# Slot 0 of a mixture-of-experts stage takes its tokens in pairs, in the down products and in the scatter

## The chip, the cores and the metric

The kernel runs on one core of a Trainium2 chip, in one launch. The metric is the device time of that launch in microseconds (us). Three runs of the kernel before took 1530.29, 1531.33 and 1532.8 us; the median is 1531.33 us. All numbers of the trace come from one profiled execution, which took 1531.39 us.

## The reference

Two layers of a transformer, 256 tokens of 1024 numbers, all in 32-bit floats. Each layer has a mixer (three kinds of attention); the first layer ends with a dense feed-forward block, the second with a mixture of eight experts, which is the part that matters here:

```python
def swiglu(h, w_gate_up, w_down):
    gt, up = jnp.split(h @ w_gate_up, 2, axis=-1)
    return (jax.nn.silu(gt) * up) @ w_down

def moe_swiglu(h, w_router, w_gate_up, w_down):
    ...
    logits = (t @ w_router).astype(jnp.float32)
    top_val, top_idx = lax.top_k(logits, TOP_K)          # TOP_K = 2 of 8
    top_w = jax.nn.softmax(top_val, axis=-1)
    ...
    for e in range(N_EXPERTS):
        y = y + combine[:, e:e + 1] * swiglu(t, w_gate_up[e], w_down[e])
```

An expert's hidden layer is 3584 wide. Its weights are 1024 x 7168 and 3584 x 1024 numbers, 44 MB; the eight of them are 352 MB, and every one is read once for each slot that works on it.

## The kernel before

**Slots.** After the router, the experts are worked on one after the other in slots. A slot is one expert with up to 96 tokens (three blocks of 32) or up to 64 (two blocks). `BLOCKS_AT = (3, 2, 3, 2, 3, 3, 2)` gives the blocks of the first seven slots; the others, in a loop, have two. A matmul with one-hot rows (`sel`) gathers a slot's tokens, and another (`selT`) scatters its result back.

**Slabs.** An expert's weights lie in memory as 42 slabs of 128 x 2048 numbers (1024 KB), in the order in which they are used. SyncE issues their transfers, in order, into a ring of 22 places (21 from slot 2 on). For slots 0 and 1 it issues one slab at a time (`single_slabs`, L683): the transfer of a slab waits on the semaphore `slab_used` until the slab 22 places before it has been used. From slot 2 on one transfer brings three slabs (L692). TensorE counts `slab_used` up with the last matmul that reads a slab.

**A slot on TensorE.** The order is written out in `expert`: gate and up products of stage 0 (8 slabs), for slot 0 then the gather of slot 1 (for the others the scatter of the slot before), gate and up of stage 1 (8), down of stage 0 (4), gate and up of stage 2 (8), down of stage 1 (4), gate and up of stage 3 (4), down of stage 2 (4), down of stage 3 (2). So 28 slabs are for gate and up, and 14 for down.

**Lanes.** A block of 32 tokens is a stationary tile of 128 x 32. Four such matmuls lie side by side in TensorE (lanes): lane g has columns 32g to 32g + 31, reads its own quarter of the slab's columns, and writes its own 32 partitions of the accumulator (`pa` for gate and up, `ps` for down). ScalarE applies SiLU (L1318), VectorE multiplies gate and up into `hs` (L1929) and transposes `hs` in 32 x 32 pieces into `hf` (L1933), which is the stationary operand of the down products.

**Pairs.** From slot 1 on, the down products take the first two blocks together: a stationary tile of 128 x 64, 512 moving columns instead of 256, and two such matmuls side by side (halves) instead of four lanes. A third block, where there is one, still goes in four lanes. The two ways need different layouts of `hs` and `hf` (`hidden_rows`, `gate_up`). With pairs, `down` takes two slabs at a time: first the pair's matmuls of both slabs, then the third block's of both, and only these last ones count `slab_used` up. Without pairs (slot 0) each slab is finished, all three blocks of it, before the next begins. The scatter has two forms in the same way: with pairs a contraction over 64 rows for the first two blocks and over 32 rows for the third; without, over 32 rows for each block. The result of slot 0 is scattered within slot 1 (`scatter_slot(1, ...)`, which asks `paired(0)`).

The function that decides is `paired(i)` at L441, called in `expert` and `choose` on VectorE, in `expert` on ScalarE, and in `down` (L2546) and `scatter_slot` (L2471) on TensorE.

Of the kernel before, what the change touches and what calls it, by code (L numbers as in the profile page):

```python
# [71 lines left out]
def blocks_of(i):  # L72
    return BLOCKS_AT[i] if type(i) is int and i < len(BLOCKS_AT) else FEW_BLOCKS
# [6 lines left out]
def is_first(i):  # L80
    return type(i) is int and i == 0


WIDE_BLOCKS, FEW_BLOCKS = 3, 2
# [89 lines left out]
def trunk(nc, x_in, mem_in, mix_norm_g, w_in, sb_q_g, sb_k_g, gla_a_up, gla_a_b, gla_o_g, ca_q_g,  # L174
# [10 lines left out]
    with ExitStack() as ctx:  # L185
# [254 lines left out]

        def paired(i):  # L441

            return not is_first(i)

        def half_rows(a, h):

# [518 lines left out]
        def _(act):  # L965
# [342 lines left out]
            def expert(i, blocks, blocks_ago, blocks_next):  # L1308
                used = i * EXP_SLABS + PRE

                if not is_first(i):
                    output(i, blocks_ago)
                for s in range(STEPS):
                    used += GU[s]
                    act.wait_ge(slab_used, used)
                    if s > 0 or not is_first(i):
                        act.wait_ge(e_turned, i * STEPS + s)
                    act.activation(hidden_rows(s, blocks, paired(i)), gate_up(s, 0, blocks, paired(i)),  # L1318
                                   ACT.Silu)\
                        .then_inc(e_silu, 1)  # L1320
                    used += DN[s - 1] if s > 0 else 0
# [14 lines left out]
        def _(dve):  # L1336
# [564 lines left out]
            def choose(i, blocks):  # L1901
                dve.wait_ge(selt_turned, i + 1)
                rows = [row_no[:, b:b + 1] for b in range(blocks)]
                for b, row in enumerate([pair_row] + rows[2:] if paired(i) else rows):
                    ins = dve.tensor_scalar(selT[:, b, :], ps[:, DM:DM + SEQ], row, None,
                                            ALU.is_equal)
                ins.then_inc(selt_ready, 1)
                name_positions(i + 1)
                if not is_first(i):
                    name_tokens(i + 1)  # L1910
# [7 lines left out]
            def expert(i, blocks, blocks_ago, blocks_next):  # L1918
                used = i * EXP_SLABS + PRE

                if not is_first(i):
                    output_lo(i, blocks_ago)
                for s in range(STEPS):
                    if s == 0 and is_first(i):
                        slot_tables()
                    used += GU[s]
                    dve.wait_ge(slab_used, used)
                    dve.wait_ge(e_silu, i * STEPS + (s + 1))
                    dve.tensor_tensor(hidden_rows(s, blocks, paired(i)), gate_up(s, 1, blocks, paired(i)),  # L1929
                                      hidden_rows(s, blocks, paired(i)), ALU.mult).then_inc(e_h, 1)  # L1930
                    dve.wait_ge(e_h, i * STEPS + (s + 1))
                    n = blocks * lanes_wide(s)
                    dve.transpose(hf[:, s % 2, 0:n], hs[:, 0:n]).then_inc(e_turned, 1)  # L1933
                    if s == 0:
                        if not is_first(i):
                            add_slot(i)
                        choose(i, blocks)
                    used += DN[s - 1] if s > 0 else 0
                turn_tokens(i + 1, blocks_next)
# [744 lines left out]
```

## Time and profile before

| what | value |
|---|---|
| median of three runs | 1531.33 us |
| the profiled execution | 1531.39 us, of which 1529.6 us between its first and its last instruction (the span) |
| slot 0 on TensorE | 729.0 to 839.9 us after the span's start |
| slot 1 on TensorE | 839.9 to 918.1 us |
| TensorE matmuls busy | 1500.2 us, 98% of the span |
| bytes moved by DMA | 482 MB, 315 GB/s over the span |

Times in the rows below are microseconds from the span's start. "Busy" for TensorE (PE) is the time in which at least one matmul was under way, so four lanes side by side count once. The trace has two records for each 32-bit matmul, and one for a matmul of type fp32r: where the program has 96 matmuls of a down stage, a row says x192. A name as "exp_raw" is the tile that holds the ring of slabs, and "exp_extra" is its 22nd place. "128*64 128x512" is a stationary tile of 128 x 64 and a moving one of 128 x 512.

### The profile page before, as it was taken

Reading aid. Unit: us, or ns where it says so; the run is one execution under the profiler, and the core shown is the slowest. Engines: PE = TensorE matmul, PEld = TensorE weight load, DVE = VectorE, ACT = ScalarE, POOL = GpSimd, SP = SyncE. Lnnn points to the kernel's source line nnn. Section 1 sums busy time; section 2 is a strip of 40 time slices with the busy share of each in tenths; the row PEclk is TensorE's granted clock in tenths of the full one; section 3 lists DMA queues with packets and bytes.
Section 4 is the critical chain, followed back from the end, with each engine's and each line's share of the span. In section 5 each row is a group of like instructions: output and inputs, shape, how many; then the busy total and the mean of one; then the engine's idle time right before and its main releaser. Section 6 shows DMA issues by size and latency. Waiting matters only on the chain.

```text
span 1529.6 us, 25846 instructions
## 1 busy us (share of the span) xinstructions
PE 1500.2 (98%) x11443; PEld 879.9 (58%) x11443; DVE 549.2 (36%) x675; ACT 431.8 (28%) x562; POOL 83.6 (5%) x126
## 2 busy tenths in 40 slices
PE   9999999999999999999999999999999999999878
PEld 7887888888888887887335333343333433433213
DVE  6655675655557664666301101001010110010101
ACT  7657653544445657453000000000000000000000
POOL 4211100200002110001000000000000000000000
PEclk9999999999999999999999999999999999999999
DMA  9655455665656554678999999999999999999996
GB/s 335 201 156 164 127 185 159 194 192 185 195 212 207 164 161 144 239 276 330 419 401 402 420 430 428 429 429 428 429 430 429 427 430 427 428 429 430 428 430 280
DMA packets 86415, 482.17 MB, mean 315 GB/s; under 512 B 11344, under 2 KB 13472, under 8 KB 64160
## 3 DMA queue, kind: packets, MB, share of 16 engines
q1 hardware_dynamic: 84784, 477.82, 80.3%
q0 software_dynamic: 1216, 2.17, 0.5%
q8 instruction: 90, 1.47, 0.4%
q10 hardware_dynamic: 304, 0.53, 0.1%
q14 instruction: 21, 0.17, 0.0%
HBM read 477.35 MB, written 3.15 MB: 314 GB/s over the span
## 4 chain that ended last, share of the span: by engine, by line
PE 89%; DMA 9%; DVE 1%; issue 0%; ACT 0%; DVEq 0%; SPq 0%; POOLq 0%
PE pa L2242 28%; PE ps L2242 19%; PE pa L2066 14%; PE pa L2068 13%; PE pa L2067 13%; DMA exp_raw<-in_moe_slabs 8%; PE ps L2236 0%; DMA w_raw<-in_w_mem_kv 0%; DMA gain<-in_mix_norm_g 0%; PE ps L1985 0%; PE ps L2415 0%; PE pa L2103 0%; PE ps L2392 0%; DVE r L1400 0%; PE ps L2025 0%
## 5 line engine op out<-in xcount | busy, mean ns | idle before, releaser
L2242 PE MATMUL pa<-exp_raw,xf 128*32 128x512 f32 (+1 forms) x5104 | 491.9, 542 | 16.6 <-DMA exp_raw<-in_moe_slabs 14.5
L2242 PEld LDWEIGHTS pa<-exp_raw,xf 128*32 128x32 f32 x5104 | 163.5, 110 | 326.1 <-issue 271.5
L1365 DVE TENSOR_TENSOR w_lo<-w_raw,w_hi 128x1024 fp32r<-128x1024 f32 x210 | 255.7, 1233 | 122.4 <-ACT w_hi L989 114.2
L989 ACT ACTIVATE w_hi<-w_raw 128x1024 fp32r<-128x1024 f32 (+1 forms) x212 | 220.1, 1053 | 130.1 <-PE pa L2068 117.6
L2242 PE MATMUL ps<-exp_raw,hf 128*32 128x256 f32 (+1 forms) x2032 | 246.7, 464 | 4.1 <-DMA exp_raw<-in_moe_slabs 4.0
L2066 PE MATMUL pa<-w_hi,r 128*128 128x512 f32 x600 | 239.7, 399 | 0.5 <-DVE r L1400 0.4
L1929 DVE TENSOR_TENSOR hs<-pa,hs 128x768 f32<-128x768 f32 (+3 forms) x32 | 23.7, 741 | 586.5 <-ACT hs L1318 586.5
L2067 PE MATMUL pa<-w_lo,r 128*128 128x512 f32 x600 | 234.0, 390 | 0.0
L2068 PE MATMUL pa<-w_hi,r 128*128 128x512 f32 x600 | 233.9, 390 | 0.0
L1318 ACT ACTIVATE hs<-pa 128x768 f32<-128x768 f32 (+3 forms) x32 | 20.4, 638 | 661.8 <-PE pa L2242 661.8
L2242 PEld LDWEIGHTS ps<-exp_raw,hf 128*32 128x32 f32 (+1 forms) x2032 | 91.6, 120 | 158.8 <-issue 128.3
L2066 PEld LDWEIGHTS pa<-w_hi,r 128*128 128x128 f32 x600 | 112.6, 188 | 27.9 <-issue 3.2
L2068 PEld LDWEIGHTS pa<-w_hi,r 128*128 128x128 f32 x600 | 112.6, 188 | 24.3
L2067 PEld LDWEIGHTS pa<-w_lo,r 128*128 128x128 f32 x600 | 112.8, 188 | 21.9
L2066 PE MATMUL pa<-w_hi,xt 128*128 128x512 f32 (+1 forms) x308 | 118.4, 384 | 0.3
L2068 PE MATMUL pa<-w_hi,xt 128*128 128x512 f32 (+1 forms) x308 | 116.6, 379 | 0.0
L2067 PE MATMUL pa<-w_lo,xt 128*128 128x512 f32 (+1 forms) x308 | 116.5, 378 | 0.0
L2066 PEld LDWEIGHTS pa<-w_hi,xt 128*128 128x128 f32 x308 | 57.9, 188 | 12.3 <-issue 1.5
L2068 PEld LDWEIGHTS pa<-w_hi,xt 128*128 128x128 f32 x308 | 57.9, 188 | 10.9
L2067 PEld LDWEIGHTS pa<-w_lo,xt 128*128 128x128 f32 x308 | 58.0, 188 | 10.3
L1914 DVE TENSOR_TENSOR yf<-ps,yf 128x768 fp32r<-128x768 f32 (+1 forms) x7 | 5.9, 844 | 85.3 <-ACT yf L1305 85.3
L1305 ACT ACTIVATE yf<-ps 128x768 fp32r<-128x768 f32 (+1 forms) x7 | 5.0, 719 | 93.3 <-PE ps L2242 93.3
(285 smaller groups left out, 856.4 us busy)
## 6 DMA issues: line engine op xcount, KB each, us to landing
exp_raw<-in_moe_slabs SPq DMA_DIRECT2D x82, 3072.0 KB, 31.0
exp_raw<-in_moe_slabs SPq DMA_DIRECT2D x86, 1024.0 KB, 8.6
w_raw<-in_w_in SPq DMA_DIRECT2D x104, 512.0 KB, 4.4
w_raw<-in_ff_w_gate_up SPq DMA_DIRECT2D x44, 512.0 KB, 4.5
w_raw<-in_ff_w_down SPq DMA_DIRECT2D x22, 512.0 KB, 4.1
w_raw<-in_w_out SPq DMA_DIRECT2D x16, 512.0 KB, 4.2
w_raw<-in_w_mem_kv SPq DMA_DIRECT2D x15, 512.0 KB, 4.6
w_raw<-in_w_br_sb SPq DMA_DIRECT2D x8, 512.0 KB, 3.3
```

The lines of the kernel that those rows point to most:

```text
L989: act.activation(dst, raw, ACT.Copy).then_inc(hi_ready, 1)
L1305: act.activation(yf[:, 0, 0:blocks * OUT], ps[:, 0:blocks * OUT], ACT.Copy)\
L1318: act.activation(hidden_rows(s, blocks, paired(i)), gate_up(s, 0, blocks, paired(i)), ACT.Silu)\
L1365: dve.tensor_tensor(dst, raw, hi.bitcast(F32), ALU.subtract)\
L1914: dve.tensor_tensor(yf[:, 1, 0:blocks * OUT], ps[:, 0:blocks * OUT], yf[:, 0, 0:blocks * OUT].bitcast(F32), ALU.subtract)\
L1929: dve.tensor_tensor(hidden_rows(s, blocks, paired(i)), gate_up(s, 1, blocks, paired(i)), hidden_rows(s, blocks, paired(i)), ALU.mult).then ...
L2066: pe.matmul(dst, hi, m_hi, start=first, stop=False)
L2067: pe.matmul(dst, hi, m_lo, start=False, stop=False)
L2068: return pe.matmul(dst, lo, m_hi, start=False, stop=last)
L2242: return pe.matmul(dst, a, b, start=start, stop=stop, skip_group_check=True)
```

## The change

One line, in the function that says for which slots tokens go in pairs:

```diff
         def paired(i):
 
-            return not is_first(i)
+            return blocks_of(i) >= FEW_BLOCKS
```

`FEW_BLOCKS` is 2 and every slot has two or three blocks, so the function is now true for all slots. It was false for slot 0 alone, which has three blocks.

On TensorE, the first down stage of slot 0 (4 slabs; "64x512" and "32x256" are the shapes of the result in the accumulator):

```order
 L2242 MATMUL pa<-exp_raw,xf 32x512 x96
-L2242 MATMUL ps<-exp_raw,hf 32x256 x48
-L2242 MATMUL ps<-exp_extra,hf 32x256 x24
-L2242 MATMUL ps<-exp_raw,hf 32x256 x24
+L2242 MATMUL ps<-exp_raw,hf 64x512 x8
+L2242 MATMUL ps<-exp_raw,hf 32x256 x16
+L2242 MATMUL ps<-exp_extra,hf 64x512 x4
+L2242 MATMUL ps<-exp_raw,hf 64x512 x4
+L2242 MATMUL ps<-exp_extra,hf 32x256 x8
+L2242 MATMUL ps<-exp_raw,hf 32x256 x8
 L2242 MATMUL pa<-exp_raw,xf 32x512 x96
```

Where 24 matmuls finished one slab, 8 of the pair form now go through two slabs, and then 16 of the lane form through the same two. The other down stages of slot 0 change alike: 336 matmuls become 56 of the pair form and 112 of the lane form, in seven groups of two slabs.

On TensorE, the scatter of slot 0's result, which stands in slot 1 between its gate and up stages:

```order
 L2613 TENSOR_LOAD slot_i
 L2613 ISA x2
 L2242 MATMUL pa<-exp_raw,xf 32x512 x64
-L2242 MATMUL ps<-yf,selT 128x256 x48
+L2242 MATMUL ps<-yf,selT 128x256 x32
 L2242 MATMUL pa<-exp_raw,xf 32x512 x16
 L2242 MATMUL ps<-ident,small 128x128 x2
```

It has 32 matmuls instead of 48: 16 contract over 64 rows, 16 over 32 rows. On ScalarE and VectorE the SiLU and the product of slot 0 write their 768 (or 384) columns in another order, with the same count of instructions, and `choose` builds `selT` for slot 0 in two instructions instead of three. GpSimd and SyncE run the same instructions as before, in the same order.

## Rows read from the trace of the kernel before

**Rows 1.** The page: GB/s moved in 40 equal slices of the span.

```profile
GB/s 335 201 156 164 127 185 159 194 192 185 195 212 207 164 161 144 239 276 330 419 401 402 420 430 428 429 429 428 429 430 429 427 430 427 428 429 430 428 430 280
```

**Rows 2.** Stretches: slot 0 after its first stage, early slot 1, later.

```profile
core 0: us, PE busy (x) PEld busy (x) DVE busy (x) ACT busy (x) POOL busy (x), PEclk, DMA share, GB/s
754.00:841.00 87.00, 87.00 (x1248) 40.30 (x1240) 5.60 (x7) 2.92 (x4) 0.00 (x0) 1.00 1.00 403
841.00:884.00 43.00, 43.00 (x400) 13.95 (x396) 7.03 (x11) 1.20 (x3) 0.00 (x0) 1.00 1.01 420
884.00:1420.00 536.00, 532.86 (x5214) 192.34 (x5208) 59.86 (x91) 17.74 (x27) 0.00 (x0) 1.00 1.00 429
```

**Rows 3.** SyncE's DMA issues, 754 to 841: waits in us, times, longest.

```profile
SPq L683 <- PE pa L2242: 44.2, 20, 4.7
SPq L683 <- PE ps L2242: 29.7, 14, 2.2
```

**Rows 4.** DMA issues, us to landing: 762-770, 804-824, 824-842, 842-884.

```profile
exp_raw<-in_moe_slabs SPq DMA_DIRECT2D x3, 1024.0 KB, 6.3
...
exp_raw<-in_moe_slabs SPq DMA_DIRECT2D x8, 1024.0 KB, 7.4
...
exp_raw<-in_moe_slabs SPq DMA_DIRECT2D x6, 1024.0 KB, 8.1
...
exp_raw<-in_moe_slabs SPq DMA_DIRECT2D x20, 1024.0 KB, 14.0
```

**Rows 5.** Timeline of TensorE, slots 0 and 1: start, us, instruction.

```profile
772.72 5.36 PE L2242 MATMUL ps<-exp_raw,hf 128*32 128x256 f32 x96
...
783.08 20.78 PE L2242 MATMUL pa<-exp_raw,xf 128*32 128x512 f32 x192
803.68 10.54 PE L2242 MATMUL ps<-exp_raw,hf 128*32 128x256 f32 x192
...
824.40 10.54 PE L2242 MATMUL ps<-exp_raw,hf 128*32 128x256 f32 x192
...
839.94 13.92 PE L2242 MATMUL pa<-exp_raw,xf 128*32 128x512 f32 x128
853.79 1.69 PE L2242 MATMUL ps<-yf,selT 32*128 32x256 f32 x48
855.42 3.64 PE L2242 MATMUL pa<-exp_raw,xf 128*32 128x512 f32 x32
```

**Rows 6.** Timeline of TensorE, slots 2 and 3.

```profile
962.38 10.97 PE L2242 MATMUL ps<-exp_raw,hf 128*64 128x512 f32 x96
973.16 20.78 PE L2242 MATMUL pa<-exp_raw,xf 128*32 128x512 f32 x192
993.87 10.97 PE L2242 MATMUL ps<-exp_raw,hf 128*64 128x512 f32 x96
...
1016.86 16.41 PE L2242 MATMUL ps<-exp_raw,hf 128*64 128x512 f32 x144
1033.09 13.92 PE L2242 MATMUL pa<-exp_raw,xf 128*32 128x512 f32 x128
1046.93 2.29 PE L2242 MATMUL ps<-yf,selT 64*128 64x256 f32 x32
1049.15 3.64 PE L2242 MATMUL pa<-exp_raw,xf 128*32 128x512 f32 x32
```

**Rows 7.** TensorE's waits for slabs, 729 to 1410, then to 1529.

```profile
PE pa L2242 <- DMA exp_raw<-in_moe_slabs: 1.1, 1, 1.1
...
PE pa L2242 <- DMA exp_raw<-in_moe_slabs: 13.4, 10, 3.3
PE ps L2242 <- DMA exp_raw<-in_moe_slabs: 4.0, 3, 1.8
```

**Rows 8.** Timeline of VectorE: the product of slot 0 and of slot 2.

```profile
773.89 0.96 DVE L1929 TENSOR_TENSOR hs<-pa,hs 128x768 f32<-128x768 f32 x1 [19.91 <-ACT hs L1318]
...
963.42 0.96 DVE L1929 TENSOR_TENSOR hs<-pa,hs 128x768 f32<-128x768 f32 x1 [15.23 <-ACT hs L1318]
```

## The prediction, made before the changed kernel ran

> **What bounds the kernel now.** First the page's row of bytes moved [rows 1]. It falls into two parts. In the first 19 slices (19 x 38.2 = 727 us) the core moves 127 to 335 GB/s; from the 20th on it moves 401 to 430 GB/s, but for the last. So the expert stage reads weights as fast as they come, and TensorE, which the table shows busy for 98% of the span, is not what sets the end there: in the last slots it waits for slabs, 13.4 + 4.0 us after 1410, and 1.1 us once before that [rows 7].
>
> Then the same view by stretches that I chose from the timeline [rows 2]. From 884 to 1420 the rate is 429 GB/s. From 841 to 884 (slot 1, still one slab per transfer) it is 420. In slot 0, from 754 to 841, it is only 403. One slab is 1.049 MB, so it takes 2.50 us at 420 GB/s and 2.60 us at 403.
>
> Why is slot 0 slower? SyncE's waits [rows 3]: in these 87 us each of the 34 transfers was held until TensorE had used the slab 22 places before, 44.2 + 29.7 us in all. The timeline of TensorE [rows 5] gives the pace of these releases. Gate and up of a stage takes 803.68 - 783.08 = 20.60 us for 8 slabs, 2.58 us each. The first down stage takes 783.08 - 772.72 = 10.36 us for 4 slabs, 2.59 us each. The last two take 839.94 - 824.40 = 15.54 us for 6 slabs, 2.59 us again. 1.049 MB in 2.59 us is 405 GB/s, which is what slot 0 moves. So in slot 0 the transfers go at TensorE's pace, and from slot 1 on, where a two-block slot uses slabs faster (839.94 to 853.79 for 8), at their own.
>
> The time from issue to landing says how much stands in the queue [rows 4]. It is 6.3 us at its lowest, 7.4 and 8.1 us later in slot 0, and 14.0 us in slot 1. I read 6.3 us as a transfer with nothing ahead of it; then q = 8.1 - 6.3 = 1.8 us at most stands ahead at the end of slot 0, and 7.7 us in slot 1. From there on TensorE can be late by some microseconds and no transfer would be late. What is lost in slot 0 is given back nowhere, since the rate is flat to the end and the last waits are for slabs.
>
> **The change, part by part.**
>
> *Matmuls of the down products.* In lanes a block's matmuls go four side by side, 256 columns each; 10.36 us for 24 such rounds is 0.43 us a round, and slot 0 has three rounds for each of its 28 chunks of 128 hidden rows. As a pair, two halves of 512 columns side by side should take what two rounds take, and the third block stays. The columns that pass are the same, so halving the count of matmuls promises nothing by itself. Slot 2 shows what it does: it also has three blocks, and it goes in pairs. Its first down stage takes 973.16 - 962.38 = 10.78 us [rows 6] against 10.36 in slot 0, and the gate and up stage behind it 993.87 - 973.16 = 20.71 against 20.60: 0.53 us more for two groups of two slabs. Its last two down stages take 1033.09 - 1016.86 = 16.23 us against 15.54: 0.69 us more for three groups. The stage between I take like the first, 0.53. Sum: 0.53 + 0.53 + 0.69 = 1.75 us for seven groups, 0.25 us each. TensorE has nothing beside it in slot 0, so all of it is on its path.
>
> What the 0.25 us are: each group changes from 64-column to 32-column tiles and back, which slot 0 did not do before. The Trainium skill says under "TensorEngine Tiling (Array Packing)", Key Properties, that changing the tiling mode, as opposed to the tile, drains TensorE. The trace agrees, with 0.12 us for each of the two changes. By that rule slot 0 gets 14 changes and is later, and without it the sum for this part would be 0.
>
> *When slabs are released.* Before, the last two slabs of a group were released 2.59 us apart. Now the pair's matmuls of both come first, and the two releases stand behind the third block of each, two rounds, 0.86 us apart. The second is late by the sum so far, the first by 1.73 us more. At the end of slot 0 that counts: if nothing is queued then, both slabs must still be moved after the first is released. Before, the last slab was moved q + 2.50 us after its release (plus a fixed time to landing); now 2 x 2.50 - 0.86 us after a release that is 1.75 us late. The difference is 1.75 + 2.50 - 0.86 - q = 3.4 - q us. With q = 1.8 it is 1.6 us, with q = 0 it is 3.4 us. Between: q = 7.4 - 6.3 = 1.1 us [rows 4] gives 2.3 us. The pairs' slower pace also eats into q before the end. I take q = 1.0, so 2.4 us. The lowest case is that the queue covers everything, 1.75 - 1.8, which is 0.
>
> *The scatter of slot 0.* In slot 1 it takes 855.42 - 853.79 = 1.63 us [rows 5]; slot 3 does the same for slot 2, in the new form, in 1049.15 - 1046.93 = 2.22 us [rows 6]. So 0.59 us more on TensorE. By then 8 slabs have been released in 13.85 us, of which 13.85 / 2.50 = 5.5 were moved, so that 2.5 slabs, some 6 us, are queued on top of q, and slabs released 0.59 us later still come in time: cost 0. If that cover were gone it would be 0.6 us.
>
> *ScalarE, VectorE.* The product of slot 0 in the old order and of slot 2 in the new one both take 0.96 us [rows 8]; one instruction of `choose` goes, whose result is wanted some 100 us later. Cost 0, and no wait of TensorE stands on either.
>
> *What follows.* TensorE is 1.75 + 0.59 = 2.34 us later in slot 1 and the transfers are 2.4 us later. The waits at the end [rows 7] stay as they are, and the end moves by the transfers' 2.4 us: 1531.39 + 2.4 = 1533.8 us. The profiled execution is 0.06 us above the median of the three runs, so nothing has to be corrected. That is 0.16% more. A measurement of this kernel can't tell less than about 0.2% (3.1 us) from no change, so this forecast counts as no change, with the sign on the slower side.
>
> **The rivals.**
>
> *The queue covers it: 1531.4 us.* If 8.1 us to landing means that 1.8 us really stand ahead, the late releases only shorten the queue in slot 0, and TensorE's own 2.34 us vanish in its 17.4 us of waits at the end [rows 7]. For it: the landings of 8.1. Against it: the rate of 403 equals the pace of release, which it wouldn't if transfers were the slower side. It also holds if the 0.25 us per group come from something of slot 2 that slot 0 lacks. Chance 20%.
>
> *Slower by more than can be missed: each group's late first release empties the queue.* Its place is the end of slot 0, its price 3.4 us with q = 0, plus up to 0.6 us if the scatter finds the queue still short: 1534.8 to 1535.4 us. It decides from q below 0.3 us on, where the sum passes 3.1 us. For it: 6.3 us in the stretch before [rows 4], and each of the seven groups takes another bite. Against it: 8.1 us just before the end. Chance 27%.
>
> *Faster, because half of the matmuls go.* A 512-column stage of 192 records takes 20.60 us, a 256-column one of as many 10.36; twice 10.36 is 20.72, so what doesn't grow with the columns is 0.12 us per 192 records. Of 3.5 such stages half the records go: 0.2 us. If the change of tile shape were free in slot 0, the end would be at 1531.2 us; if down products then fell below 2.50 us a slab, at most 14 x (2.59 - 2.50) = 1.3 us come off, 1530.1. Chance 6%, most of it still within 0.2%. (The Trainium skill, "TensorEngine Tiling (Array Packing)", Instruction Overhead, gives about 60 cycles for each matmul; for 168 matmuls fewer that would be an estimate of 4.2 us one after the other, or 1.05 us four side by side. The 0.12 us per 192 records don't bear it out here, because the overhead of one lane lies beside another's work.)
>
> **How the numbers follow.** The forecast of 1533.8 has 47%, its own range is 1533.0 to 1534.6 (q from 1.8 to 0.2). Slower by over 0.2% means above 1534.4: the 27% and some 4% of the forecast's upper edge, 31%. Faster by over 0.2% means below 1528.3, which no sum here reaches; 5% for what I don't see. The rest, 64%, is within 0.2%. The range of 1531.0 to 1535.6 us takes in the covered case below and the emptied queue above.
>
> **What would show it.** In the new profile the first down stage of slot 0 should take 10.8 us and the last two 16.2, slot 1 should begin 1.7 to 1.9 us later, and the scatter should take 2.2 us. GB/s of slot 0 should fall from 403 to about 395, those of 884 to 1420 stay at 429. The waits for slabs after 1410 should stay near 17 us: if they shrink by 2 us, the queue covered the change; if they stay and the end moves by over 3 us, the late first release did more than I took. If the down stages take 10.36 us as before, the reading of slot 2 was wrong.

## The result and the profile after

The changed kernel takes 1534.02 us (median of 21 runs, 1532.81 to 1536.7), the one before 1531.07 us (21 runs on the same chips, 1530.24 to 1532.8). The ratio is 1.0022, with a 95% interval of 1.0016 to 1.0028: slower by 2.95 us, or about 0.2%, with an interval that lies wholly above 1. The profiled execution of the changed kernel took 1532.92 us, 1.53 us more than that of before; why this is less than the medians' 2.95 us is taken up with the ninth experiment.

TensorE in slot 0 and slot 1 of the changed kernel, from its timeline (start, us, instruction), against [rows 5]:

```profile
728.80 20.78 PE L2242 MATMUL pa<-exp_raw,xf 128*32 128x512 f32 x192
...
783.40 20.78 PE L2242 MATMUL pa<-exp_raw,xf 128*32 128x512 f32 x192
804.11 10.97 PE L2242 MATMUL ps<-exp_raw,hf 128*64 128x512 f32 x96
...
825.37 10.97 PE L2242 MATMUL ps<-exp_raw,hf 128*64 128x512 f32 x96
...
841.60 13.92 PE L2242 MATMUL pa<-exp_raw,xf 128*32 128x512 f32 x128
855.45 2.29 PE L2242 MATMUL ps<-yf,selT 64*128 64x256 f32 x32
857.66 3.64 PE L2242 MATMUL pa<-exp_raw,xf 128*32 128x512 f32 x32
```

The gate and up stage behind the first down stage takes 804.11 - 783.40 = 20.71 us, 0.11 more than before, and the last two down stages 841.60 - 825.37 = 16.23 us against 15.54. Slot 1 begins at 841.60, 1.66 us later, though slot 0 began 0.2 us earlier: slot 0 takes TensorE 841.6 - 728.8 = 112.8 us, and before 839.9 - 729.0 = 110.9, so it is 1.9 us longer. The scatter takes 857.66 - 855.45 = 2.21 us against 1.63. These are the durations of slot 2 and slot 3 of before [rows 6], almost to the hundredth.

The stretches of the same three windows as in [rows 2] (us, busy time of each engine, TensorE's clock, DMA share, GB/s):

```profile
754.00:841.00 87.00, 87.00 (x888) 31.71 (x884) 5.61 (x7) 2.11 (x3) 0.00 (x0) 1.00 0.99 394
841.00:884.00 43.00, 43.00 (x384) 14.19 (x380) 7.15 (x11) 2.00 (x3) 0.00 (x0) 1.00 1.01 418
884.00:1420.00 536.00, 533.39 (x5226) 192.43 (x5220) 59.85 (x91) 17.73 (x27) 0.00 (x0) 1.00 1.01 429
```

Slot 0 moves 394 GB/s instead of 403. 9 GB/s over 87 us are 0.78 MB, or 1.9 us at 420 GB/s. From 841 to 884 the rate is 418 instead of 420, and behind 884 it is 429 as before: nothing is seen to be given back (over 536 us a difference of 1 GB/s would be 1.2 us; the ninth experiment has a closer reading). Time to landing in the last stretch of slot 0 (first row: the ring's places, second: its 22nd place), against 8.1 us in [rows 4]:

```profile
exp_raw<-in_moe_slabs SPq DMA_DIRECT2D x6, 1024.0 KB, 7.4
exp_extra<-in_moe_slabs SPq DMA_DIRECT2D x1, 1024.0 KB, 6.2
```

It falls to 7.4 and 6.2 us: less stands in the queue. Earlier in slot 0 two transfers, issued at 777.33 and 782.78, land sooner still:

```profile
exp_raw<-in_moe_slabs SPq DMA_DIRECT2D x1, 1024.0 KB, 5.0
exp_extra<-in_moe_slabs SPq DMA_DIRECT2D x1, 1024.0 KB, 4.9
```

So a slab with little or nothing ahead of it takes 4.9 us, and not the 6.3 us that the prediction took for it. TensorE's waits for slabs, 729 to 1410, then 1410 to 1531 (us in total, times, longest):

```profile
PE pa L2242 <- DMA exp_raw<-in_moe_slabs: 0.6, 1, 0.6
```

```profile
PE pa L2242 <- DMA exp_raw<-in_moe_slabs: 14.3, 9, 2.8
PE ps L2242 <- DMA exp_raw<-in_moe_slabs: 2.3, 3, 1.8
```

14.3 + 2.3 = 16.6 us after 1410, against 17.4 [rows 7]. TensorE still runs out of slabs in the last slots, so the transfers set the end in both kernels, and TensorE's own lateness has hardly eaten into the waits.

### The profile page after: what moved, and what is told of

Read it like the earlier page. It is cut to its first block, busy times and chain, and to the rows that moved or that the text cites. A ratio compares the mean times of both kernels' runs of the same rounds, so it can differ in the third digit from the quotient of the medians.

```text
span 1531.0 us, 25141 instructions
## 1 busy us (share of the span) xinstructions
PE 1502.6 (98%) x11091; PEld 872.2 (57%) x11091; DVE 549.2 (36%) x674; ACT 431.7 (28%) x562; POOL 83.2 (5%) x126
## 3 DMA queue, kind: packets, MB, share of 16 engines
q0 software_dynamic: 1216, 2.17, 0.4%
HBM read 477.35 MB, written 3.15 MB: 314 GB/s over the span
## 4 chain that ended last, share of the span: by engine, by line
PE 87%; DMA 11%; DVE 1%; issue 0%; ACT 0%; DVEq 0%; POOL 0%; ACTq 0%; SPq 0%
PE pa L2242 26%; PE ps L2242 18%; PE pa L2066 14%; PE pa L2067 13%; PE pa L2068 13%; DMA exp_raw<-in_moe_slabs 10%; PE ps L2236 0%; DMA w_raw<-in_w_mem_kv 0%; PE ps L1985 0%; DVE w_lo L1355 0%; PE ps L2415 0%; PE pa L2103 0%; PE ps L2392 0%; DVE r L1400 0%; PE ps L2025 0%
## 5 line engine op out<-in xcount | busy, mean ns | idle before, releaser
L2242 PE MATMUL ps<-exp_raw,hf 128*64 128x512 f32 (+1 forms) x1744 | 248.0, 490 | 2.4 <-DMA exp_raw<-in_moe_slabs 2.3
L1929 DVE TENSOR_TENSOR hs<-pa,hs 128x768 f32<-128x768 f32 (+3 forms) x32 | 23.7, 741 | 587.0 <-ACT hs L1318 587.0
L2242 PEld LDWEIGHTS ps<-exp_raw,hf 128*64 128x64 f32 (+1 forms) x1744 | 85.0, 123 | 165.9 <-issue 145.8
L2067 PEld LDWEIGHTS pa<-w_lo,r 128*128 128x128 f32 x600 | 112.8, 188 | 21.9
```

The source lines that it names most:

```text
L2067: pe.matmul(dst, hi, m_lo, start=False, stop=False)
L2242: return pe.matmul(dst, a, b, start=start, stop=stop, skip_group_check=True)
```

## The experiments

Theory A, the prediction's: while slot 0 runs, the transfers stand close behind TensorE's releases, so both its slower pace and the late first release of a group delay them; from slot 1 on the queue is deep, and the delay stays to the end. Against it: B, the queue covers slot 0 and the cost comes from TensorE's work elsewhere; C, the late first release is all; P, the pace is all. Each kernel ran on one chip with runs of the kernel before beside it; differences are of medians.

| experiment | us against before | ratio, 95% interval |
|---|---|---|
| 1 lanes, late release | 1532.70 - 1531.01 = +1.69 | 1.0011 (1.0002 to 1.0020) |
| 2 lanes, filler | 1532.92 - 1531.01 = +1.91 | 1.0010 (1.0001 to 1.0019) |
| 3 pairs, one slab | 1534.16 - 1531.01 = +3.15 | 1.0022 (1.0013 to 1.0031) |
| 4 late gather | 1532.87 - 1531.01 = +1.86 | 1.0013 (1.0004 to 1.0022) |
| 5 third block first | 1533.39 - 1530.85 = +2.54 | 1.0017 (1.0008 to 1.0026) |
| 6 filler in slot 2 | 1531.37 - 1530.85 = +0.52 | 1.0003 (0.9994 to 1.0012) |
| 7 filler behind the scatter | 1531.42 - 1530.85 = +0.57 | 1.0003 (0.9994 to 1.0013) |
| 8 half slabs | 1531.05 - 1530.85 = +0.20 | 1.0001 (0.9992 to 1.0010) |
| 9 the change again | 1533.68 - 1530.78 = +2.90 | 1.0020 (1.0011 to 1.0029) |
| 10 pairs, four slabs | 1534.98 - 1530.78 = +4.20 | 1.0027 (1.0017 to 1.0038) |
| 11 no third block | 1528.61 - 1530.78 = -2.17 | 0.9987 (0.9978 to 0.9996) |
| 12 triples early | 1530.32 - 1530.78 = -0.46 | 0.9996 (0.9987 to 1.0005) |

**1. The late release without pairs.**

```diff
-                    each = 2 if paired(i) else 1
+                    each = 2
...
-                                for b in range(2 if paired(i) else 0, blocks):
+                                for b in range(2, blocks):
```

> Edit: the kernel before (slot 0 in lanes, no change of tile shape, old scatter), but its down products also go through two slabs at a time, the third block last, so that the first slab of each group is released 1.73 us later. TensorE's time in slot 0 stays as before (10.36 us for the first down stage). Theory A (transfers of slot 0 follow its releases: the end moves by the late release of the last slabs, less the queue): 1.64 us less a queue of 0 to 1.5 us, so +0.1 to +1.6 us, I expect +0.6. Theory C (the late first release is the whole cost, the changes of tile shape nothing): +2 to +3 us, as the change itself. Theory B (the queue covers slot 0, and the cost comes from TensorE's later work): 0.

(Ahead of this loop, which ends with the release, a second loop of the same kind goes through blocks 0 and 1 of both slabs.) Its timeline at the end of slot 0: the first two blocks of two slabs, then their third block, then slot 1.

```profile
824.22 10.54 PE L2242 MATMUL ps<-exp_raw,hf 128*32 128x256 f32 x192
834.58 1.91 PE L2242 MATMUL ps<-exp_extra,hf 128*32 128x256 f32 x32
836.30 1.91 PE L2242 MATMUL ps<-exp_raw,hf 128*32 128x256 f32 x32
838.03 1.05 PE L2242 MATMUL ps<-exp_extra,hf 128*32 128x256 f32 x16
838.89 1.05 PE L2242 MATMUL ps<-exp_raw,hf 128*32 128x256 f32 x16
839.76 13.92 PE L2242 MATMUL pa<-exp_raw,xf 128*32 128x512 f32 x128
```

From 824.22 to 839.76 it takes 15.54 us, as before. The last two releases are at the ends of the rows from 838.03 and 838.89 on, 0.86 us apart instead of 2.59. TensorE does no more work in slot 0, and still the kernel is 1.69 us slower: the late release costs by itself. That is at the upper end of what theory A allowed (1.64 us with an empty queue), and less than C said, though the interval (0.3 to 3.1 us) doesn't rule C out; B and P, which say 0, fall.

**2. The pace without pairs.**

```diff
+                                if q % 2 == 0:
+                                    for g in range(LANES):
+                                        mm(lane(pa, g)[:, 3 * BW:3 * BW + 152], hf[:, s % 2, 0:LANE],
+                                           exp_slots[place(i, j)][:, g * OUT:g * OUT + 152], True, True)
```

> Edit: the kernel before, with four more matmuls of 152 columns side by side ahead of each two slabs of slot 0's down products, written to a bank that nobody reads: about 0.26 us for each of seven groups, 1.8 us in all, with each slab still released by itself. Theory A: the transfers are late by what TensorE is late, less the queue: +0.5 to +1.8 us, I expect +1.3. Theory C: 0 to +0.3. Theory B: 0.

One filler, and the start of slot 1:

```profile
836.55 0.44 PE L2242 MATMUL pa<-exp_extra,hf 128*32 128x152 f32 x8
836.81 2.77 PE L2242 MATMUL ps<-exp_extra,hf 128*32 128x256 f32 x48
...
841.99 13.92 PE L2242 MATMUL pa<-exp_raw,xf 128*32 128x512 f32 x128
```

A filler takes 836.81 - 836.55 = 0.26 us. The cost of 1.91 us is about what TensorE lost, 7 x 0.26 = 1.8 us, but its interval is wide (0.2 to 2.9 us). So the pace costs by itself too. C, which said 0 to 0.3 us, is at the very edge of that interval; it falls with the third experiment. The two parts together would be 3.6 us; the change costs 2.95, which the intervals allow.

**3. Pairs, one slab at a time.**

```diff
-                    each = 2 if paired(i) else 1
+                    each = 1 if is_first(i) else 2
```

> Edit: the changed kernel, but slot 0 goes through its down slabs one at a time (pair form, then third block, then the release), so twice as many changes of tile shape (28) and no late first release. TensorE's down products should take 14 x 0.25 = 3.5 us more than before. Theory A: +2.5 to +3.5 us over before, about as much as the change or a little more. Theory C: under +1 us. Theory B: the 0.6 us of the scatter at most.

```profile
804.81 11.54 PE L2242 MATMUL ps<-exp_raw,hf 128*64 128x512 f32 x96
816.17 10.54 PE L2242 MATMUL pa<-exp_raw,xf 128*32 128x256 f32 x192
826.64 11.54 PE L2242 MATMUL ps<-exp_raw,hf 128*64 128x512 f32 x96
```

This down stage of four slabs and the gate and up stage behind it take 826.64 - 804.81 = 21.83 us, 1.11 us more than the 824.40 - 803.68 = 20.72 in lanes [rows 5]; the changed kernel's took 825.37 - 804.11 = 21.26, 0.54 more. So twice the changes of tile shape take about twice the time: 1.11 us for eight, 0.54 for four, some 0.14 us each. +3.15 us lies in the range that A gave (2.5 to 3.5); C said under 1, which is outside the interval (2.0 to 4.8 us), so C falls.

**4. A later gather (a miss).**

```diff
                 if is_first(i):
                     turn_choice(i)
-                    gather(1, blocks_next)
...
-                    if s == STEPS - 1 and not is_first(i):
+                    if s == STEPS - 1:
```

> Edit: the kernel before, but slot 0 gathers slot 1's tokens ahead of its fourth gate and up stage, as all other slots do, and no longer behind the first. TensorE's work is the same, but the slabs of the stages between are released 1.7 us earlier. Theory A (slot 0's transfers stand close to the releases): -0.5 to -1.1 us. Theory B (the queue covers them anyway): 0.

Faster was expected, and it is 1.86 us slower. Its timeline: the second gate stage, and the start of slot 1.

```profile
749.55 0.71 PE L2242 MATMUL ps<-ident,small 128*128 128x128 f32 x4
751.61 20.81 PE L2242 MATMUL pa<-exp_raw,xf 128*32 128x512 f32 x192 [1.35 <-DVE hs L1929]
...
841.18 4.05 PE L2242 MATMUL pa<-exp_raw,xf 128*32 128x512 f32 x36
```

With the gather gone from its place, TensorE waits 1.35 us there for VectorE's product (L1929), which the gather had covered; slot 0 then ends at 841.18, 1.24 us later than before. My premise that TensorE's work stays the same was wrong, and the miss fits theory A: more time of TensorE in slot 0, about as much at the end.

**5. The third block first.**

```diff
+                        if is_first(i):
+                            for m, q in enumerate(qs):
+                                wait_slab(pe, i, j + m)
...
+                                            ins = mm(lane(ps, g)[:, b * OUT:(b + 1) * OUT],
...
+                            for m, q in enumerate(qs):
...
+                                        ins = mm(half_rows(ps, h)[:, 0:BW], hf[:, s % 2, at:at + PAIR],
...
+                                ins.then_inc(slab_used, 1)
```

> Edit: the changed kernel, but in slot 0 the third block goes first through the two slabs of a group and the pair form behind it, so that the two releases are 1.73 us apart instead of 0.86. The changes of tile shape stay at 14 and TensorE's slot 0 stays 1.75 us longer than before. Theory A (releases of slot 0, pace and lumps together): up to 0.9 us faster than the changed kernel, so +2.1 to +2.9 us over before. Theory C (the lump is all): +1 us or less. Theory P (the pace is all): as the changed kernel, +2.9.

+2.54 us lies where A put it, and is 0.4 us less than the change. That is the direction one expects when the two releases of a group are further apart, but too small a difference for these intervals to show.

**6 and 7. The same work outside slot 0.** In the sixth, two rounds of filler ahead of each two slabs of slot 2; in the seventh, two rounds behind the scatter in slot 1:

```diff
+                            if m == 0 and type(i) is int and i == 2:
+                                for g in tuple(range(LANES)) * 2:
+                                    mm(lane(pa, g)[:, 3 * BW:3 * BW + 152], ident[:, 0:LANE],
+                                       hn[:, 0, g * OUT:g * OUT + 152], True, True)
```

```diff
                     scatter_slot(i, blocks_ago)
+                    if type(i) is int and i == 1:
+                        for g in tuple(range(LANES)) * 2:
+                            mm(lane(pa, g)[:, 3 * BW:3 * BW + 176], ident[:, 0:LANE],
+                               hn[:, 0, g * OUT:g * OUT + 176], True, True)
```

> Edit: the kernel before, with eight more matmuls of 152 columns, two rounds of four, ahead of each two slabs of slot 2's down products: about 0.5 us for each of seven groups, 3.6 us of TensorE in all, twice what the change adds to slot 0, at a place where slabs stand in the queue for some 26 us. Theory A: no change, 0 +- 0.5 us. Theory B (TensorE's time counts wherever it is): +1.7 to +3.6 us.

> Edit: the kernel before, with eight more matmuls of 176 columns behind the scatter of slot 0's result in slot 1, two rounds, 0.6 us, the size of the change's dearer scatter and at its place. Theory A: 0 +- 0.3 us. Theory B (the scatter counts): +0.6 us.

Slot 2 with the fillers of the sixth, of which the first and the third are shown, and the start of slot 3:

```profile
962.21 0.70 PE L2242 MATMUL pa<-hn,ident 128*32 128x152 f32 x16
962.84 5.52 PE L2242 MATMUL ps<-exp_raw,hf 128*64 128x512 f32 x48
...
974.14 20.78 PE L2242 MATMUL pa<-exp_raw,xf 128*32 128x512 f32 x192
994.74 0.70 PE L2242 MATMUL pa<-hn,ident 128*32 128x152 f32 x16
...
1036.65 5.76 PE L2242 MATMUL pa<-exp_raw,xf 128*32 128x512 f32 x52
```

A filler's row takes 962.84 - 962.21 = 0.63 us, but the gate and up stage ahead of the next one is 0.11 us shorter than in [rows 6] (994.74 - 974.14 = 20.60 against 20.71): the change to the pair's tile shape now stands behind the filler, so a filler adds 0.52 us. From the first filler to slot 3 it is 1036.65 - 962.21 = 74.44 us against 1033.09 - 962.38 = 70.71; without the 0.11 us that only moved, TensorE lost 3.6 us there, as I had worked out. The kernel is 0.52 us slower, with an interval from -0.9 to 1.8 us. Engine time that is paid about in full in slot 0 costs little or nothing in slot 2. B falls. The seventh can't be told from 0, nor from the 0.6 us that were added: the scatter's share stays open at 0 to 0.6 us.

**8. Releases in halves (a miss).**

```diff
+                        sp.wait_ge(half_used, HALF_SLABS.index(n) + 1)
+                        sp.dma_start(dst[:, 0:DM], src[:, 0:DM]).then_inc(first_ready[n % FIRST_RAW], 16)
+                        sp.wait_ge(slab_used, i * EXP_SLABS + (PRE + j + 1 - FIRST_RAW))
+                        sp.dma_start(dst[:, DM:], src[:, DM:]).then_inc(first_ready[n % FIRST_RAW], 16)
```

> Edit: the kernel before, but the last six slabs of slot 0 (its third and fourth down stages) are released in halves: a count after the first 128 rows of the slab, and the transfer that takes its place is issued as two of 512 KB, the first of them 1.3 us earlier. TensorE's work is the same. Theory A (at the end of slot 0 the transfers stand close behind the releases): -0.5 to -1.2 us, faster than both kernels. Theory B (the queue covers slot 0): 0, or up to +0.3 us for smaller transfers.

Nothing that can be told came of it: +0.20 us, with an interval from -1.2 to 1.5 us, in which the whole of A's range (-0.5 to -1.2) still lies. Its stretches before and under the half slabs, and then the same two of the kernel before:

```profile
824.00:833.00 9.00, 9.00 (x172) 5.46 (x168) 1.73 (x3) 0.49 (x1) 0.00 (x0) 1.00 0.98 376
833.00:846.00 13.00, 13.00 (x196) 6.00 (x187) 0.96 (x1) 0.81 (x1) 0.00 (x0) 1.00 1.03 411
```

```profile
824.00:833.00 9.00, 9.00 (x172) 5.43 (x168) 1.73 (x3) 0.49 (x1) 0.00 (x0) 1.00 0.99 393
833.00:846.00 13.00, 13.00 (x193) 6.03 (x188) 0.96 (x1) 0.81 (x1) 0.00 (x0) 1.00 0.99 398
```

From 833 on it moves 411 GB/s instead of 398, which over 13 us is 0.4 us gained, and from 824 to 833 it moves 376 instead of 393, 0.4 us lost. Theory A's gain from earlier releases is not borne out by this run, and not ruled out either.

**9. The change again.** The same kernel as the changed one, for a second profile.

> The changed kernel once more, with a profile of its own, because its timed median (+2.95 us) and its profiled execution (+1.53 us against the profiled one of before) differ. If the change costs what the transfers lose in slot 0 and no more, its profile shows slab transfers 1.7 to 2.9 us late from slot 1 to the end, and the timed runs +2.2 to +3.3 us. If there is a second cost at the end of the program, the lateness grows after 1410 us.

Timed, it repeats: +2.90 us. Its profiled execution took 1533.68 us, 0.76 us more than the other profile of the same kernel. Slot 0's last stages and slot 1's start, and then the stretch from 820 to 846 in this execution, in the other one of the changed kernel, and in that of before:

```profile
825.57 10.97 PE L2242 MATMUL ps<-exp_raw,hf 128*64 128x512 f32 x96
...
841.80 13.92 PE L2242 MATMUL pa<-exp_raw,xf 128*32 128x512 f32 x128
```

```profile
820.00:846.00 26.00, 26.00 (x292) 10.54 (x284) 2.69 (x4) 1.30 (x2) 0.00 (x0) 1.00 0.97 372
```

```profile
820.00:846.00 26.00, 26.00 (x292) 10.52 (x284) 2.69 (x4) 1.30 (x2) 0.00 (x0) 1.00 0.99 389
```

```profile
820.00:846.00 26.00, 26.00 (x436) 13.83 (x429) 2.69 (x4) 1.30 (x2) 0.00 (x0) 1.00 0.99 399
```

TensorE takes 841.80 - 825.57 = 16.23 us, the same as in the other profile. But the transfers move 372 GB/s here and 389 there: 17 GB/s over 26 us are 0.44 MB, 1.1 us. The last slab that waits for a release of slot 0 is issued 0.4 us behind slot 1's start in all three executions, at 840.33 (before), 841.98 and 842.18 (this one). Its time to landing, in this order:

```profile
exp_raw<-in_moe_slabs SPq DMA_DIRECT2D x1, 1024.0 KB, 8.0
exp_raw<-in_moe_slabs SPq DMA_DIRECT2D x1, 1024.0 KB, 7.8
exp_raw<-in_moe_slabs SPq DMA_DIRECT2D x1, 1024.0 KB, 8.5
```

So it lands at 848.3, 849.8 and 850.7, 1.5 and 2.4 us later than before. The spans are 1529.6, 1531.0 and 1531.9 us: 1.4 and 2.3 us longer. What these two executions lose by the end of slot 0 is what they lose at their end, and no second cost after 1410 shows. The 0.9 us between the two profiles of the changed kernel come from slot 0's transfers, with TensorE's stages equal, and the first profile was one of the faster executions. Whether the rest of the spread (3.9 us from the fastest run to the slowest, 2.6 before) has the same source, no run here shows.

**10. Pairs, four slabs at a time.**

```diff
-                    each = 2 if paired(i) else 1
+                    each = 4 if is_first(i) else 2
```

> Edit: the changed kernel, but slot 0 goes through four slabs at a time (the pair form of all four, then the third block of all four): eight changes of tile shape instead of 14, 1.0 us of TensorE instead of 1.75, but the first slab of a group of four is released some 5 us later than slab by slab. If the changes of tile shape are all that counts: +1.0 us over before. Theory A (pace and late releases both count): +2 to +4 us, no better than the change.

```profile
803.78 10.68 PE L2242 MATMUL ps<-exp_raw,hf 128*64 128x512 f32 x96
814.28 10.54 PE L2242 MATMUL pa<-exp_raw,xf 128*32 128x256 f32 x192
824.75 10.68 PE L2242 MATMUL ps<-exp_raw,hf 128*64 128x512 f32 x96
```

```profile
754.00:841.00 87.00, 87.00 (x900) 32.76 (x896) 5.61 (x7) 2.17 (x4) 0.00 (x0) 1.00 0.95 384
```

The down stage of four slabs takes 814.28 - 803.78 = 10.50 us, only 0.14 us more than in lanes and 0.28 less than in groups of two; with the stage behind it, 824.75 - 803.78 = 20.97 us, it is 0.25 us more for its two changes. So fewer changes of tile shape do save TensorE's time. And yet this kernel has the highest median of all, +4.20 us, just above what A had put as its upper end: the first slab of a group is released later still. In slot 0 the DMA share falls to 0.95 and the rate to 384 GB/s: 19 GB/s less than before, over 87 us, are 1.65 MB, or 3.9 us at 420 GB/s. Its interval (2.6 to 5.8 us) overlaps with the change's, so it isn't shown to be slower than the change; but it rules out the +1.0 us that the changes of tile shape alone would cost. With the first experiment it is the plainest evidence that the releases, and not TensorE's time alone, set the cost.

**11. Less work in slot 0.** The third block's down products are left out but for the first 128 hidden rows, so the output lacks them.

```diff
-                                for b in range(2 if paired(i) else 0, blocks):
+                                for b in range(2 if paired(i) else 0,
+                                               2 if is_first(i) and (s > 0 or k > 0) else blocks):
```

> Edit: the kernel before without the third block of slot 0's down products, but for the first 128 hidden rows; it leaves that part of the computation out. TensorE is done with slot 0 27 x 0.43 = 11.7 us earlier. Theory A (TensorE's releases hold the transfers of slot 0 back): they then move at up to 420 GB/s instead of 403, which over 87 us is 3.5 us, so -2.5 to -3.5 us. Theory B (the queue covers slot 0, transfers set the pace already): 0 to -0.5 us.

Start of slot 1, then the stretches of slot 0 up to about the first slab that is released earlier and from there on, in this kernel and in that of before, and landing at the end of slot 0's stretch:

```profile
828.18 13.92 PE L2242 MATMUL pa<-exp_raw,xf 128*32 128x512 f32 x128
```

```profile
754.00:776.00 22.00, 22.00 (x240) 7.67 (x236) 1.94 (x2) 0.81 (x1) 0.00 (x0) 1.00 1.01 397
776.00:841.00 65.00, 65.00 (x904) 29.12 (x896) 4.63 (x6) 2.11 (x3) 0.00 (x0) 1.00 1.01 419
```

```profile
754.00:776.00 22.00, 22.00 (x244) 7.58 (x236) 1.94 (x2) 0.81 (x1) 0.00 (x0) 1.00 1.01 402
776.00:841.00 65.00, 65.00 (x1012) 32.72 (x1008) 3.67 (x5) 2.11 (x3) 0.00 (x0) 1.00 1.00 403
```

```profile
exp_raw<-in_moe_slabs SPq DMA_DIRECT2D x9, 1024.0 KB, 20.2
```

Slot 0 ends at 828.18, 11.8 us earlier, and a transfer then takes 20.2 us from issue to landing instead of 8.1. From 776 on the rate is 419 GB/s instead of 403, all but the 420 of slot 1: 16 GB/s over 65 us are 1.04 MB or 2.5 us, less some 0.3 us for the 397 ahead of it. The end is 2.17 us earlier, a little less than the 2.5 that A gave as its least; A had counted all of the 87 us, though releases come earlier only from about 775 on. So TensorE does hold slot 0's transfers back in the kernel before, by some 2 us, and what TensorE saves beyond that is worth nothing.

**12. Slot 1's later slabs three by three.** The rows show 420 GB/s in slot 1 and 429 from slot 2 on, both with a deep queue [rows 2, 4]; the last 18 slabs of slot 1 now come in six transfers.

```diff
+                        sp.wait_ge(slab_used, i * EXP_SLABS + (PRE + j + LOAD - FIRST_RAW))
+                        sp.dma_start(exp_raw[:, at:at + LOAD, :].rearrange("p a n -> p (a n)"),
+                                     moe_slabs[bass.ds(e, 1), j // LOAD]
```

> Edit: the kernel before, but the last 18 slabs of slot 1 come three by three in one transfer, as those of slot 2 and later do, instead of one by one. By the rows a slab takes 2.50 us at 420 GB/s and 2.44 us at 429, and in slot 1 the queue is deep: 18 x 0.06 = 1.1 us. If transfers bound the program from there on, as I read it: -0.7 to -1.2 us, faster than both kernels. If not: 0.

```profile
841.00:884.00 43.00, 43.00 (x400) 13.97 (x396) 7.03 (x11) 1.20 (x2) 0.00 (x0) 1.00 1.01 426
```

From 841 to 884 the rate is 426 instead of 420, which over 43 us is 0.6 us. The median is the lowest of all complete kernels, 0.46 us under that of before and less than the 0.7 us expected, but the interval includes no change: it is faster than the changed kernel, and isn't shown to be faster than the one before.

## Why the prediction was right in its time, and what in its sum was not

1533.8 us was forecast and 1534.02 measured, inside the range. That the two times are only 0.2 us apart is in part luck: 2.4 us was forecast on top of 1531.39, and 2.95 us was measured on top of 1531.07. The steps:

- *Slot 0 in pairs costs what slot 2 shows*: right. 16.23 us for the last two down stages was forecast as 16.2, 2.21 us for the scatter as 2.2. The sum of 1.75 us left out the gate and up stage ahead of the first down stage, whose end also grows by 0.11 us; 1.9 us was measured for all of slot 0. The Trainium skill's rule ("TensorEngine Tiling (Array Packing)", Key Properties: a change of tiling mode drains TensorE) agrees with the third and tenth experiments: 0.25 us for two changes of tile shape, 0.54 for four, 1.11 for eight.
- *Halving the matmuls promises nothing*: right; the stages got longer with half the instructions.
- *Transfers of slot 0 go at TensorE's pace, and the loss stays*: right in the sign and the place, by experiments 2, 6, 9 and 11; in the eleventh the transfers, once no longer held back, reached 419 GB/s, close to the 420 that the prediction took as their own rate. It was not that the DMA engines stood idle until a release came: in slot 0 of the kernel before their share is 1.00 [rows 2], and the time to landing grew from 6.3 to 8.1 us [rows 4], so the transfers were even a little slower than the releases. Why a slab takes longer there, no run shows.
- *The late first release, 3.4 - q us in all with q = 1.0*: that a late first release costs was right (experiments 1 and 10). The term q, what stands ahead in the queue and covers it, was not. It was worked out from 6.3 us to landing with nothing ahead; the changed kernel has slabs that land 4.9 us after issue, so by the same reading 8.1 - 4.9 = 3.2 us stood ahead, and the formula would give 0.2 us. The change cost 2.95 us, as if q were 0.45; the first experiment alone cost 1.69 us where the formula gives 1.64 - q, as if q were 0. So what stands ahead covers little or nothing of a late release, and that q = 1.0 came near the measured cost is luck.
- *The scatter is hidden*: not contradicted, but not shown.
- *No change within 0.2%, 64%*: 0.19% over 1531.07 us was measured, which the ratio gives as 0.22%, with an interval on both sides of 0.2%, so neither side of it is shown. But 0.2% was too coarse as the least that can be told: the interval reaches only 0.06% to either side, and no change is outside it. I gave the emptied queue 27%; with a queue that covers next to nothing, more would have been due.

The rivals: "the queue covers it" fell with experiments 1, 2 and 11, "faster, because half of the matmuls go" with the timeline. "The emptied queue" was nearly it: a late first release that is hardly covered, with 2.95 instead of 3.4 us.

What stays open: why the transfers respond differently in two executions with the same releases, why slabs take longer in slot 0 while the DMA engines are busy, and whether earlier releases of the last six slabs gain anything. That late releases and a slower TensorE in slot 0 lengthen its transfers is shown; how they do it is not.

## What to carry to other kernels

Where a ring of buffers feeds a program that is bound by its transfers, look for the stretch in which the consumer is the slower side, even by 3 or 4% (2.59 us a slab here, against 2.50 with a deep queue): there a microsecond of the consumer costs about as much at the end (1.8 us cost 1.9), and buffers handed back late cost too (1.7 us without any more work), while 3.6 us of the consumer elsewhere cost nothing that could be told. A grouping that saves instructions but hands buffers back in bunches can cost more than it saves, so read when a buffer is released, not only how long the work takes. And before work is moved out of a gap, ask what it covers there.

## What the runs showed of the hardware that I had not expected

- Two executions of one kernel, with TensorE's stages equal to 0.01 us, moved 389 and 372 GB/s in the same 26 us, where little stood in the queue (the stretches of the ninth experiment). Where the queue was deep, from 884 to 1420, the rate was 429 in both kernels.
- The time of a change of tile shape shows at the end of the row ahead of it. With fillers in slot 2 the gate and up stage took 20.60 us instead of 20.71, and the filler's row of eight matmuls 0.63 us (962.21 to 962.84), 0.11 more than twice the 0.26 us of four in slot 0 (836.55 to 836.81). In slot 0 two changes cost 0.25 us (tenth experiment), four 0.54 (the change), eight 1.11 (third).
- A slab of 1024 KB landed 4.9 us after issue where the queue had run short (782.78, changed kernel), 8.0 us at the end of slot 0 of the kernel before, and 20.2 us where releases ran ahead (eleventh experiment).
